# The act tiles of the experts' down pass move from SyncE's DMA queue to ScalarE's

## The chip, the cores and the metric

One Trainium2 chip, one of its cores. The metric is the device time of one execution in microseconds (us), as the median of several runs. Engines are named as in the profile: PE is TensorE (matmul), PEld its weight load, DVE VectorE, ACT ScalarE, POOL GpSimd, SP SyncE; SPq is SyncE's own row of issued transfers.

## The reference, cut to what matters

The program computes three transformer blocks one after the other on 512 tokens of width 1024. The change lies in the second block's feed-forward layer, a layer of 16384 experts of which every token picks 16 for each of 8 heads:

```python
def block(args):
    hb, ib, gb = args
    act = jax.nn.gelu(jnp.einsum('pd,phkd->phk', hb, expert_u[ib]))
    return jnp.einsum('phk,phkd->pd', gb.astype(hb.dtype) * act, expert_v[ib])
```

## The kernel before

For 384 of the 512 tokens the kernel works densely. The 16384 experts form 128 tiles of 128 experts. `experts_up` computes gelu(u h) of all experts of a tile for the 384 tokens and stores it as an act tile of 128 x 384 float32 in DRAM (`acts`), and it stores a matrix of gates (`gates`), zero where a token didn't pick an expert. `experts_down`, the stage of the change, then walks over the 128 tiles and sums V tile (128 experts x 1024) times (act tile x gates) in PSUM. For the other 128 tokens it gathers rows of V by index: GpSimd issues 128 indirect transfers, one for each of 128 picked slots, and VectorE adds each into `sums`, about one in a tile's time.

For tile n of `experts_down` the engines do the following, in this order on each.

- ScalarE waits for V tile n and for PE to be done with tile n-2, casts V into `v.hi`, waits for `product` of tile n, casts it into `w.hi`.
- VectorE waits for act tile n (and the gates of its group of 8 tiles) and multiplies them into `product` (L2426); it then waits for `v.hi` and computes the rest `v.lo` (helper line L71), then waits for `w.hi` and computes `w.lo` (L71), and then adds one gathered row (L2409).
- PE waits for `v.lo` and `w.lo` and makes 8 x 3 matmuls of 384 columns (L2385).
- SyncE waits for `v_ready` of tile n, fetches V tile n+3 into the slot that has come free, then act tile n+3; after every eighth tile it fetches the gates of a whole group of 8 tiles, two groups ahead. V tiles, act tiles and gates stand in one queue, in that order of issue.

The ring of V tiles has three slots (`picked.tables`), that of act tiles three (`act_ring`), that of gates two (`gate_ring`). A V tile is waited for on one of three semaphores (`v_landed`), an act tile on one of three (`act_landed`). The gates' transfer reads pieces of 1024 bytes, an act tile's reads pieces of 1536 bytes, a V tile's pieces of 4096 bytes. The fetches stand in these lines of the kernel before:

```python
nc.sync.dma_start(self.tables[:, (n + NKEYS) % 3, :], self.p.dram["peer_v"][n]).then_inc(self.v_landed[n % 3], 16)
nc.sync.dma_start(act_ring[:, n % RING3, :], acts[n]).then_inc(act_landed[n % RING3], 16)
```

Ahead of the loop SyncE issues act tile 0, the gates of tiles 0 and 1, act tiles 1 and 2, the gates of tiles 2 to 7 and those of the second group; V tiles 0 to 2 are fetched by the stage before.

Of the kernel before, what the change touches and what calls it, by code (L numbers as in the profile page):

```python
# [880 lines left out]
NKEYS = 128  # L881
# [220 lines left out]
def second_block(p, x, mod):  # L1102

    nc, d = p.nc, p.dram
    with ExitStack() as ctx:
# [25 lines left out]
        with ExitStack() as c:  # L1131
# [8 lines left out]
            gates = nc.dram_tensor("peer_gates", (LOTS, P, NKEYS, LOT_TOKENS), F32, kind="Internal").ap()  # L1140
            experts_up(p, h2, scores, acts, gates, picked)
        experts_down(p, acts, gates, x, gt2, picked)


# [1167 lines left out]
def experts_down(p, acts, gates, x, gate, picked):  # L2312
# [3 lines left out]
    nc, d = p.nc, p.dram  # L2316
    RING3 = 3
    with ExitStack() as ctx:
        ring, landed = picked.tables, picked.v_landed
        act_ring = p.sb(ctx, "act_ring", [P, RING3, DENSE])  # L2320
# [7 lines left out]
        act_landed = p.sems(ctx, *[f"act_landed{u}" for u in range(RING3)])  # L2328
        gate_landed = p.sems(ctx, "gate_landed0", "gate_landed1")
        v_hi_ready, v_ready, multiplied, w_hi_ready, w_ready, tile_done, added = p.sems(  # L2330
            ctx, "v_hi_ready", "v_ready", "multiplied", "w_hi_ready", "w_ready", "tile_done", "added")
# [10 lines left out]
        def slot(n):  # L2342
            return ring[:, (n + NKEYS) % RING3, :]

        def fetch_act(n):
            nc.sync.dma_start(act_ring[:, n % RING3, :], acts[n]).then_inc(act_landed[n % RING3], 16)

        def fetch_gates(m, first, last, landed_):
            nc.sync.dma_start(gate_ring[:, m % 2, :, first:last, :], gates[:, :, m * GATE_TILES + first:m * GATE_TILES + last, :]
                              .rearrange("l p a t -> p l a t")).then_inc(landed_, 16)  # L2350
# [9 lines left out]
        @block.sync  # L2360
        def _(sp):
            for n in range(NKEYS - RING3):
                sp.wait_ge(v_ready, n + 1)
                picked.fetch_v(n + RING3)
                sp.wait_ge(multiplied, n + 1)
                fetch_act(n + RING3)
                m = n // GATE_TILES
                if n % GATE_TILES == GATE_TILES - 1 and m + 2 < NKEYS // GATE_TILES:
                    fetch_gates(m + 2, 0, GATE_TILES, gate_landed[m % 2])

        @block.gpsimd
# [20 lines left out]
        @block.scalar  # L2392
        def _(act):
            nc.scalar.activation(share[:], picked.pre[:], ACT.Gelu_apprx_tanh).then_inc(gelu_ready, 1)
            for n in range(NKEYS):
                act.wait_ge(landed[n % RING3], 16 * (n // RING3 + 1))
                if n >= 2:
                    act.wait_ge(tile_done, n - 1)
                nc.scalar.activation(v.hi[:, n % 2, :], slot(n), ACT.Copy).then_inc(v_hi_ready, 1)  # L2399
                act.wait_ge(multiplied, n + 1)  # L2400
                nc.scalar.activation(w.hi[:, n % 2, :], product[:, n % 2, :], ACT.Copy).then_inc(w_hi_ready, 1)

        @block.vector
        def _(dve):
# [846 lines left out]
```

## Time and profile before

| | us |
|---|---|
| median of 3 runs | 4329.05 |
| lowest and highest | 4323.47, 4330.01 |
| profiled execution, its own time | 4340.69 |
| span of the profiled execution | 4338.9 |
| first and last matmul of the changed stage's sum, from the span's start | 2544.5, 3124.5 |
| PE busy over the span | 3790.5 (87%) |

The span runs from the first to the last instruction of the profiled execution; it lies 1.8 us under that execution's own time, and that execution was 11.6 us longer than the median of the runs. Times in rows are counted from the span's start. An idle time in square brackets stands at the instruction that ended it, with the engine or transfer that released it.

### The profile page before, as it was taken

Reading aid. Unit: us, or ns where it says so; the run is one execution under the profiler, and the core shown is the slowest. Engines: PE = TensorE matmul, PEld = TensorE weight load, DVE = VectorE, ACT = ScalarE, POOL = GpSimd, SP = SyncE. Lnnn points to the kernel's source line nnn. Section 1 sums busy time; section 2 is a strip of 40 time slices with the busy share of each in tenths; the row PEclk is TensorE's granted clock in tenths of the full one; section 3 lists DMA queues with packets and bytes.
Section 4 is the critical chain, followed back from the end, with each engine's and each line's share of the span. In section 5 each row is a group of like instructions: output and inputs, shape, how many; then the busy total and the mean of one; then the engine's idle time right before and its main releaser. Section 6 shows DMA issues by size and latency. Waiting matters only on the chain. (4 is left out here: it accounts for less than half of the span.)

```text
span 4338.9 us, 51551 instructions
## 1 busy us (share of the span) xinstructions
PE 3790.5 (87%) x19109; PEld 3261.0 (75%) x19109; DVE 2528.5 (58%) x4080; ACT 1207.0 (28%) x2101; POOL 348.2 (8%) x276
## 2 busy tenths in 40 slices
PE   7998977799986988889999979999877879779998
PEld 6876764478755787689999979999856848566876
DVE  4544778454434563369999867777643436654433
ACT  1101122121012232233578833333221122412300
POOL 0000011000000020002212212222100000000000
PEclk9999978799998989999999989999988979889999
DMA  3222710222211001238889889998612101021232
GB/s 140 97 71 82 255 60 1 95 74 96 73 64 58 29 1 40 87 119 271 293 291 330 307 302 329 324 336 314 220 58 73 51 33 67 1 78 68 87 104 71
DMA packets 198386, 590.94 MB, mean 136 GB/s; under 512 B 22448, under 2 KB 80688, under 8 KB 196016
## 3 DMA queue, kind: packets, MB, share of 16 engines
q1 hardware_dynamic: 161344, 454.38, 30.3%
q0 software_dynamic: 36864, 134.23, 8.7%
q8 instruction: 106, 1.74, 0.2%
q14 instruction: 72, 0.59, 0.0%
HBM read 536.11 MB, written 52.43 MB: 136 GB/s over the span
## 5 line engine op out<-in xcount | busy, mean ns | idle before, releaser
L350 DVE CAST w_hi<-w_ring 128x1024 fp32r<-128x1024 f32 (+1 forms) x336 | 238.5, 710 | 644.0 <-PE banks L315 495.8
L71 DVE TENSOR_TENSOR w_lo<-w_ring,w_hi 128x1024 fp32r<-128x1024 f32 (+1 forms) x336 | 424.5, 1263 | 11.5
L315 PE MATMUL banks<-x_hi,w_hi 128*128 128x512 f32 x896 | 355.8, 397 | 46.9 <-DVE x_lo L71 46.8
L2385 PE MATMUL out_ps<-w_hi,v_hi 128*128 128x384 f32 x1024 | 349.2, 341 | 45.5 <-DVE w_lo L71 45.5
L2085 PE MATMUL up_ps<-h_hi,u_hi 128*128 128x384 f32 x1024 | 351.4, 343 | 21.2 <-DVE u_lo L71 21.2
L315 PE MATMUL banks<-x_lo,w_hi 128*128 128x512 f32 x896 | 354.4, 396 | 0.0
L315 PE MATMUL banks<-x_hi,w_lo 128*128 128x512 f32 x896 | 354.2, 395 | 0.0
L2385 PE MATMUL out_ps<-w_hi,v_lo 128*128 128x384 f32 x1024 | 347.6, 339 | 0.0
L2385 PE MATMUL out_ps<-w_lo,v_hi 128*128 128x384 f32 x1024 | 347.6, 339 | 0.0
L2085 PE MATMUL up_ps<-h_lo,u_hi 128*128 128x384 f32 x1024 | 343.8, 336 | 0.0
L2085 PE MATMUL up_ps<-h_hi,u_lo 128*128 128x384 f32 x1024 | 343.6, 336 | 0.0
L315 PE MATMUL banks<-h_hi,w_hi 128*128 128x512 f32 x576 | 235.3, 408 | 48.5 <-DVE w_lo L71 24.2
L315 PE MATMUL banks<-hidden_hi,w_hi 128*128 128x512 f32 x608 | 239.9, 395 | 20.0 <-DVE w_lo L71 20.0
L315 PE MATMUL banks<-hidden_lo,w_hi 128*128 128x512 f32 x608 | 239.2, 393 | 0.0
L315 PE MATMUL banks<-hidden_hi,w_lo 128*128 128x512 f32 x608 | 238.8, 393 | 0.0
L315 PEld LDWEIGHTS banks<-x_hi,w_hi 128*128 128x128 f32 x896 | 169.6, 189 | 91.7 <-DVE w_lo L71 28.8
L2385 PEld LDWEIGHTS out_ps<-w_hi,v_hi 128*128 128x128 f32 x1024 | 196.6, 192 | 50.4 <-DVE v_lo L71 50.4
L315 PE MATMUL banks<-hn_hi,w_hi 128*128 128x264 f32 (+1 forms) x704 | 186.4, 324 | 52.6 <-DVE w_lo L71 45.2
L2399 ACT ACTIVATE v_hi<-expert_tiles 128x1024 fp32r<-128x1024 f32 x128 | 135.7, 1060 | 345.4 <-PE out_ps L2385 260.9
L315 PE MATMUL banks<-h_lo,w_hi 128*128 128x512 f32 x576 | 231.7, 402 | 0.0
L315 PE MATMUL banks<-h_hi,w_lo 128*128 128x512 f32 x576 | 231.0, 401 | 0.0
L2085 PEld LDWEIGHTS up_ps<-h_hi,u_hi 128*128 128x128 f32 x1024 | 193.7, 189 | 25.9 <-DVE u_lo L71 25.7
(532 smaller groups left out, 7812.0 us busy)
## 6 DMA issues: line engine op xcount, KB each, us to landing
expert_tiles<-peer_u SPq DMA_DIRECT2D x128, 512.0 KB
expert_tiles<-peer_v SPq DMA_DIRECT2D x128, 512.0 KB
w_ring<-w_in SPq DMA_DIRECT2D x104, 512.0 KB, 3.6
w_ring<-ffn_up SPq DMA_DIRECT2D x88, 512.0 KB, 3.5
w_ring<-w_ff SPq DMA_DIRECT2D x64, 512.0 KB, 3.8
ada_ring<-w_ada SPq DMA_DIRECT2D x48, 512.0 KB, 5.2
peer_acts<-act_ring SPq DMA_DIRECT2D x128, 192.0 KB
peer_gates<-staging SPq DMA_DIRECT2D x12, 2048.0 KB
```

Source lines behind the costliest of these rows:

```text
L71: return nc.vector.tensor_tensor(self.lo[at], value, self.hi[at].bitcast(F32), ALU.subtract)
L315: last = nc.tensor.matmul(banks[:, j, s, 0:n], a[:, u % 2, k, :], b[:, g * kg + k, x_from + c:x_from + c + n], start=(g == 0 and k == 0 an ...
L350: nc.vector.tensor_copy(w_parts.hi[:, u % 2], ring[:, u % slots]).then_inc(hi_ready, 1)
L2085: last = nc.tensor.matmul(up_ps[:, n % 3, 0:DENSE], a[:, n % 2, k, :], b[:, k, P:T], start=(k == 0 and part_ == 0), stop=(k == DB - 1 and ...
L2385: last = nc.tensor.matmul(out_ps[:, b, P:T], a[:, n % 2, b * P:b * P + P], r[:, n % 2, :], start=(n == 0 and part == 0), stop=(n == NKEYS ...
L2399: nc.scalar.activation(v.hi[:, n % 2, :], slot(n), ACT.Copy).then_inc(v_hi_ready, 1)
```

## The change

SyncE no longer fetches act tiles inside the loop. ScalarE issues the fetch of act tile n+3 right behind its cast of `product` of tile n, for which it has already waited until `product` n was computed, so that the slot is free. V tiles and gates stay on SyncE, and SyncE waits for `multiplied` only ahead of the gates. The act tiles 0 to 2 stay on SyncE. No computation is changed.

```diff
@@ -2362,10 +2362,9 @@
             for n in range(NKEYS - RING3):
                 sp.wait_ge(v_ready, n + 1)
                 picked.fetch_v(n + RING3)
-                sp.wait_ge(multiplied, n + 1)
-                fetch_act(n + RING3)
                 m = n // GATE_TILES
                 if n % GATE_TILES == GATE_TILES - 1 and m + 2 < NKEYS // GATE_TILES:
+                    sp.wait_ge(multiplied, n + 1)
                     fetch_gates(m + 2, 0, GATE_TILES, gate_landed[m % 2])
@@ -2399,6 +2398,8 @@
                 nc.scalar.activation(v.hi[:, n % 2, :], slot(n), ACT.Copy).then_inc(v_hi_ready, 1)
                 act.wait_ge(multiplied, n + 1)
                 nc.scalar.activation(w.hi[:, n % 2, :], product[:, n % 2, :], ACT.Copy).then_inc(w_hi_ready, 1)
+                if n + RING3 < NKEYS:
+                    nc.scalar.dma_start(act_ring[:, n % RING3, :], acts[n + RING3]).then_inc(act_landed[n % RING3], 16)
```

On SyncE, around one fetch of gates (`gate_ring`), the kernel before issues:

```order
L1895 DMA expert_tiles<-peer_v 128x1024
L2346 DMA act_ring<-peer_acts 128x384
L2349 DMA gate_ring<-peer_gates 128x12x256
L1895 DMA expert_tiles<-peer_v 128x1024
L2346 DMA act_ring<-peer_acts 128x384
L1895 DMA expert_tiles<-peer_v 128x1024
L2346 DMA act_ring<-peer_acts 128x384
```

At the same place the changed kernel issues on SyncE (x8 stands for eight equal rows):

```order
L1895 DMA expert_tiles<-peer_v 128x1024 x8
L2349 DMA gate_ring<-peer_gates 128x12x256
L1895 DMA expert_tiles<-peer_v 128x1024 x8
```

The act tiles have left SyncE's queue; the gates stand directly behind a V tile, and the next V tile directly behind the gates.

On ScalarE, in the middle of the stage, two tiles of the kernel before read:

```order
L2399 ACTIVATE v_hi<-expert_tiles 128x1024
L2401 ACTIVATE w_hi<-product 128x384
L2399 ACTIVATE v_hi<-expert_tiles 128x1024
L2401 ACTIVATE w_hi<-product 128x384
```

and two tiles of the changed kernel, whose lines are numbered by its own file:

```order
L2398 ACTIVATE v_hi<-expert_tiles 128x1024
L2400 ACTIVATE w_hi<-product 128x384
L2402 DMA act_ring<-peer_acts 128x384
L2398 ACTIVATE v_hi<-expert_tiles 128x1024
L2400 ACTIVATE w_hi<-product 128x384
L2402 DMA act_ring<-peer_acts 128x384
```

ScalarE has one more instruction in a tile, between its cast of `product` and its next cast of V. The order on PE, VectorE and GpSimd is the same as before.

## Rows read from the trace of the kernel before

**Rows 1.** The page's head and part 1, the whole span.

```profile
span 4338.9 us, 51551 instructions
PE 3790.5 (87%) x19109; PEld 3261.0 (75%) x19109; DVE 2528.5 (58%) x4080; ACT 1207.0 (28%) x2101; POOL 348.2 (8%) x276
```

**Rows 2.** Who waited for whom, 2530 to 3140: total us, times, longest.

```profile
ACT v_hi L2399 <- PE out_ps L2385: 260.9, 96, 5.0
ACT v_hi L2399 <- DMA expert_tiles<-peer_v: 84.3, 28, 7.3
...
DVE product L2426 <- DMA act_ring<-peer_acts: 58.0, 15, 6.7
PEld out_ps L2385 <- DVE v_lo L71: 50.4, 17, 15.2
...
DVE sums L2409 <- DMA gathered<-peer_v,expert_ids: 4.1, 1, 4.1
```

**Rows 3.** Two bursts to the next; columns: engines' busy, PEclk, DMA, GB/s.

```profile
2689.60:2727.60 38.00, 34.78 (x192) 34.49 (x192) 26.85 (x33) 12.00 (x16) 8.01 (x8) 0.96 0.92 319
2762.80:2797.70 34.90, 33.30 (x192) 33.01 (x192) 26.53 (x33) 12.00 (x16) 8.01 (x8) 1.00 0.95 328
```

**Rows 4.** SyncE's timeline around one fetch of gates: start, us taken to issue.

```profile
2762.05 0.43 SPq L2346 DMA_DIRECT2D act_ring<-peer_acts  x1
2762.82 0.39 SPq L2349 DMA_DIRECT2D gate_ring<-peer_gates  x1
2765.83 2.39 SPq L1895 DMA_DIRECT2D expert_tiles<-peer_v  x1
2768.27 0.49 SPq L2346 DMA_DIRECT2D act_ring<-peer_acts  x1
```

**Rows 5.** The same burst in stretches of 2 us; columns as in rows 3.

```profile
2764.00:2766.00 2.00, 2.00 (x14) 2.00 (x13) 1.42 (x2) 0.89 (x2) 0.59 (x1) 1.00 0.78 250
...
2776.00:2778.00 2.00, 2.00 (x13) 2.00 (x12) 0.00 (x0) 0.07 (x1) 0.94 (x1) 1.00 1.02 402
```

**Rows 6.** ScalarE's timeline, three bursts, with the idle time before each.

```profile
2706.96 1.06 ACT L2399 ACTIVATE v_hi<-expert_tiles 128x1024 fp32r<-128x1024 f32 x1 [6.97 <-DMA expert_tiles<-peer_v]
...
2742.28 1.06 ACT L2399 ACTIVATE v_hi<-expert_tiles 128x1024 fp32r<-128x1024 f32 x1 [3.98 <-DMA expert_tiles<-peer_v]
...
2764.38 0.51 ACT L2401 ACTIVATE w_hi<-product 128x384 fp32r<-128x384 f32 x1
2767.57 1.06 ACT L2399 ACTIVATE v_hi<-expert_tiles 128x1024 fp32r<-128x1024 f32 x1 [2.69 <-PE out_ps L2385]
...
2777.93 1.06 ACT L2399 ACTIVATE v_hi<-expert_tiles 128x1024 fp32r<-128x1024 f32 x1 [4.72 <-DMA expert_tiles<-peer_v]
```

**Rows 7.** VectorE's timeline at the same three bursts.

```profile
2707.49 0.56 DVE L2426 TENSOR_TENSOR product<-act_ring,gate_ring 128x384 f32<-128x384 f32 x1 [4.92 <-DMA act_ring<-peer_acts]
...
2744.11 0.56 DVE L2426 TENSOR_TENSOR product<-act_ring,gate_ring 128x384 f32<-128x384 f32 x1 [3.23 <-DMA act_ring<-peer_acts]
...
2779.25 0.56 DVE L2426 TENSOR_TENSOR product<-act_ring,gate_ring 128x384 f32<-128x384 f32 x1 [3.46 <-DMA act_ring<-peer_acts]
```

**Rows 8.** PE's weight loads that ended three pauses.

```profile
2565.27 0.29 PEld L2385 LDWEIGHTS out_ps<-w_hi,v_hi 128*128 128x128 f32 x1 [5.05 <-DVE v_lo L71]
...
2709.93 0.19 PEld L2385 LDWEIGHTS out_ps<-w_hi,v_hi 128*128 128x128 f32 x1 [3.51 <-DVE v_lo L71]
...
2781.53 0.19 PEld L2385 LDWEIGHTS out_ps<-w_hi,v_hi 128*128 128x128 f32 x1 [1.89 <-DVE v_lo L71]
```

**Rows 9.** PE and PEld at L2385 behind the last two pauses, PEclk, DMA, GB/s.

```profile
2710.00:2720.00 10.00, 10.00 (x49) 10.00 (x50) 0.83 0.84 276
2781.60:2791.60 10.00, 10.00 (x58) 10.00 (x59) 1.00 0.92 322
```

**Rows 10.** Transfers issued in the stage, with the size of each.

```profile
act_ring<-peer_acts SPq DMA_DIRECT2D x128, 192.0 KB
gate_ring<-peer_gates SPq DMA_DIRECT2D x15, 1536.0 KB
```

## The prediction

> **What bounds the kernel now.** I read the page's engine shares first: PE is busy for 87% of the span [rows 1], so only what PE waits for counts. Then the stage of the change alone, by its table of waits. PE's weight loads waited 50.4 us there, all of it for `v_lo` [rows 2]; the longest, 15.2 us, ends at the stage's first matmul, which leaves 35.2 us between tiles. That is the reachable idle time, 0.8% of the kernel. One step back the table names the cause: ScalarE waited 84.3 us for V tiles and VectorE 58.0 us for act tiles, while the gathered rows, which travel in GpSimd's own queue, were late once, by 4.1 us [rows 2]. When nothing is late, ScalarE waits for PE (260.9 us, 96 times [rows 2]), and a tile takes 4.16 us of PE (8 tiles take 33.3 us, PE's busy time in the second of [rows 3]).
>
> The timelines then show where the 35 us lie. There are 14 fetches of gates in the loop and one pause of PE behind each, plus one of 5.05 us at tile 3 [rows 8], where two sets of gates are under way at once. The 14 pauses add up to 29.4 us, 1.0 to 3.5 us each, the longest of them in [rows 8]. [Rows 4] show one: the gates (1536 KB) are issued at 2762.82, and the V tile behind them in the queue at 2765.83. That V tile starts ScalarE's cast at 2777.93 [rows 6], 12.1 us after its issue, and PE resumes at 2781.53 [rows 8]. The granted clock is the second price of a pause. Behind the pause of 1.89 us it stayed at 1.00 and 59 weight loads ran in 10 us; behind the one of 3.51 us it was 0.83 in the mean, so part of the time at the lower level, 1.2 GHz, and only 50 loads ran [rows 9]. Nine loads of 0.17 us (10 us over 59) are 1.5 us. This happened behind 5 of the 14 pauses, and 38.0 us against 34.9 us from one fetch of gates to the next is what it and the longer pause make together [rows 3].
>
> **What the change removes: the lateness of act tiles.** In the loop `product` stands ahead of `v_lo` on VectorE, so a late act tile holds `v_lo`. But `v_lo` also needs ScalarE's 1.06 us cast of V, and only what `product` ends after that cast counts (a hand-over of 0.1 us taken off). At the three bursts of [rows 6, 7]:
> - 2707.49 + 0.56 = 2708.05 against 2706.96 + 1.06 + 0.1 = 2708.12: nothing.
> - 2744.67 against 2743.44: 1.23 us.
> - 2779.81 against 2779.09: 0.72 us.
> The same subtraction at all 14 bursts gives 7.7 us, 0.55 us each, and 1.05 us at tile 3. So of the 58.0 us of waiting for act tiles only 8.7 us held PE; the rest ran beside the wait for V, which the change leaves behind the gates. This is the first point that I want seen: the V tile that is late stands in the same place of the same queue as before.
>
> **What it adds: act tiles that overtake.** During a burst the DMA engines are full: their share is 1.02, at 402 GB/s, late in the burst [rows 5]. An act tile is 192 KB [rows 10], 196,608 bytes, so 0.49 us at 400 GB/s (my estimate from these rows). Before, the late V tile n+4 had act tile n+3 ahead of it in the queue, and acts n+4, n+5 and n+6 behind it. Now ScalarE issues act n+4 behind its cast at 2764.38, act n+5 one tile later and act n+6 two tiles later, at about 2773, all before the V tile lands at 2777.9 [rows 6]. They compete with it: +0.49, +0.49, and for the last, which meets only the V tile's end, half, +0.25. Act n+3 leaves the burst, since it is issued about 1.6 us sooner (behind the cast of `product` instead of behind `v_lo`), where the engines have room (share 0.78, 250 GB/s just after the gates are issued [rows 5]): -0.49. SyncE comes to the gates one issue of 0.43 us sooner [rows 4]; I count half of it, since what goes ahead of the gates at that time is not full bandwidth: -0.2. Sum for V: +0.54 us a burst. The bounds are 0 (the acts fit into the unused share at the start of the burst) and +0.98 (all three in full, no gain from the earlier gates).
>
> **The rest of the edit** I cost at nothing. ScalarE issues 125 transfers of about the 0.43 us that SyncE takes for one [rows 4]; the 2.69 us for which ScalarE then waits for PE covers it [rows 6]. If that cover is gone, it is 0.43 us a tile, but it is gone only right behind a pause, where the next cast of V may start 0.4 us late and PE has a whole tile of 4.16 us in hand. No transfer is issued by ScalarE in this trace, so there's no row for it; the bounds are 0.1 us and SyncE's blocked issue of 2.39 us [rows 4], which 2.69 us still cover. SyncE's removed waits cost nothing: it issues and waits on, and of what it issues only V matters.
>
> **The sum.** 14 x 0.54 = +7.6 us for V, -7.7 us for acts; at tile 3, +1.5 us (three acts overtake) - 1.05 us = +0.4 us; clock unchanged. Together +0.3 us. The profiled execution would go from 4340.69 to 4341; the median of the runs is 11.6 us lower, and I put the change on it: 4329 us. What a measurement of this kernel can tell from no change is about 0.2%, 8.7 us, so 4320.4 and 4337.7 are the borders.
>
> The Trainium skill, DMA: Bandwidth & Descriptors, section "Issuing engines are not separate DMA queues", says that transfers issued by different engines share the same 16 DMA engines and interleave, and that using several only saves issue time. By that rule alone the sum is 0, 4329 us; no run here shows it yet for ScalarE's queue. It speaks against a gain from bandwidth, not against a gain from order.
>
> **The rivals.**
> - Faster: the acts hide in the unused share at the head of the burst, V lands when it did, and all of the acts' lateness is gone. For it: 0.78 of the share used for 2 us [rows 5], which at 400 GB/s leaves room for 0.3 MB, one and a half act tiles. Against: acts n+5 and n+6 come when the share is full. It gives -8.7 us and spares the slower clock behind one or two pauses (-1.5 to -3): 4329 - 11 = 4318 us. Chance 0.22. It decides where V is later by less than 0.1 us a burst.
> - Slower: the overtaking acts cost V their full price, 0.98 us a burst. For it: the gathered rows in their own queue are hardly ever late [rows 2], so a queue of its own does win over SyncE's backlog, and the loser is the V tile that all wait for. 14 x 0.98 - 7.7 + 0.4 = +6.4 us, and longer pauses bring the slower clock behind three more, +4.5 us: 4340 us. Chance 0.17. It decides from about 0.8 us a burst. The skill's page of above, section "Queues, rings and completion order", says that each DMA engine goes round its queues in turn, a packet from each; by that rule acts would pass the gates' backlog, as this rival says.
> - Slower by ScalarE: if its issue blocks behind the gates for longer than SyncE's 2.39 us, v_hi is late before the pause comes. Beyond the 2.69 us each us is paid once a burst, at most about 1 us: 4329 + 14 = 4343 us. Against: SyncE's blocked issue is of its own queue's backlog. Chance 0.05.
> - Nothing changes: acts stay behind the gates also from the other queue, both landings as before: 4329 us. Chance 0.08. My forecast, the wash, has 0.48.
>
> **How the numbers follow.** Wash and nothing make 0.56 for within 0.2%; faster 0.22; slower 0.17 + 0.05 = 0.22. The range takes in both main rivals with their bounds: 4314 to 4342 us. It leaves out somewhat under 2 in 10: a gain of more than the 8.7 us and the clock, and a blocking ScalarE.
>
> **What would show it.** In the changed trace the wait of `product` for act tiles should be near nothing, and that of `v_hi` for V tiles should grow from 84.3 us by 5 to 10 us, with as many pauses of PE as before, behind the gates, 27 to 32 us in 14. If V's wait stays or falls, the faster rival holds; if PE's pauses pass 36 us, the slower. ScalarE waiting for PE for less than 200 us would show that its issue isn't free. I am wrong most easily in V's landing: it is set by the slowest of 16 engines, and 0.3 us a burst either way is 4 us.

## The result, and the profile after

The changed kernel is slower by half a per cent: its median is 4352.61 us against 4330.81 us before, 12 runs each, ratio 1.0049 with a 95% interval of 1.0036 to 1.0062. The prediction was 4329 us in a range of 4314 to 4342.

The page of the changed kernel, its head, part 1 and the queues of part 3:

```profile
span 4352.7 us, 51551 instructions
PE 3797.2 (87%) x19109; PEld 3271.8 (75%) x19109; DVE 2529.1 (58%) x4080; ACT 1204.9 (28%) x2101; POOL 351.1 (8%) x276
...
q1 hardware_dynamic: 143344, 429.80, 29.1%
q0 software_dynamic: 36864, 134.23, 8.7%
q10 hardware_dynamic: 18000, 24.58, 1.8%
```

Against [rows 1], PE is busy for 6.7 us more and its weight loads for 10.8 us more, with as many instructions; the other engines stay within 3 us. A third queue, q10, now carries 18000 packets and 24.58 MB: the 125 act tiles that ScalarE fetches.

The table of waits of the changed kernel, 2530 to 3160 (total us, times, longest):

```profile
ACT v_hi L2398 <- PE out_ps L2384: 273.9, 96, 6.7
DVE v_lo L71 <- ACT v_hi L2398: 168.0, 106, 6.8
ACT v_hi L2398 <- DMA expert_tiles<-peer_v: 100.5, 27, 8.4
PEld out_ps L2384 <- DVE v_lo L71: 64.5, 17, 15.4
...
DVE sums L2410 <- DMA gathered<-peer_v,expert_ids: 4.1, 1, 4.1
```

Against [rows 2], the wait of `product` for act tiles is gone altogether; that of `v_hi` for V tiles has grown from 84.3 to 100.5 us (the prediction had 5 to 10 us more), and PE's wait for `v_lo` from 50.4 to 64.5 us.

The same stretch as in the second of [rows 3], and a later one, in the changed kernel (from one fetch of gates to the next; engines' busy, PEclk, DMA share, GB/s):

```profile
2768.70:2808.20 39.50, 36.26 (x194) 35.97 (x193) 26.77 (x34) 11.89 (x16) 8.11 (x8) 0.91 0.86 295
...
2843.40:2878.30 34.90, 33.48 (x194) 33.19 (x193) 26.73 (x34) 11.89 (x16) 8.10 (x8) 1.00 0.98 348
```

The first took 34.9 us before and takes 39.5 now, with 0.91 of the clock; the later one is as long as that row of before. So the change hurts some bursts much more than others.

The first of them step by step. SyncE's timeline of the changed kernel (start, us taken to issue):

```profile
2768.28 0.33 SPq L1895 DMA_DIRECT2D expert_tiles<-peer_v  x1
2768.66 0.43 SPq L2349 DMA_DIRECT2D gate_ring<-peer_gates  x1
2772.44 0.33 SPq L1895 DMA_DIRECT2D expert_tiles<-peer_v  x1
```

ScalarE's timeline, same kernel:

```profile
2770.43 0.33 ACTq L2402 DMA_DIRECT2D act_ring<-peer_acts  x1
...
2774.59 0.33 ACTq L2402 DMA_DIRECT2D act_ring<-peer_acts  x1
...
2778.34 1.06 ACT L2398 ACTIVATE v_hi<-expert_tiles 128x1024 fp32r<-128x1024 f32 x1 [2.69 <-PE out_ps L2384]
2778.75 0.33 ACTq L2402 DMA_DIRECT2D act_ring<-peer_acts  x1
2779.31 0.51 ACT L2400 ACTIVATE w_hi<-product 128x384 fp32r<-128x384 f32 x1
2786.81 1.06 ACT L2398 ACTIVATE v_hi<-expert_tiles 128x1024 fp32r<-128x1024 f32 x1 [7.00 <-DMA expert_tiles<-peer_v]
```

VectorE's:

```profile
2782.32 0.55 DVE L2427 TENSOR_TENSOR product<-act_ring,gate_ring 128x384 f32<-128x384 f32 x1
...
2787.97 1.23 DVE L71 TENSOR_TENSOR v_lo<-expert_tiles,v_hi 128x1024 fp32r<-128x1024 f32 x1 [5.10 <-ACT v_hi L2398]
```

And PE's weight loads:

```profile
2789.78 0.28 PEld L2384 LDWEIGHTS out_ps<-w_hi,v_hi 128*128 128x128 f32 x1 [3.53 <-DVE v_lo L71]
2789.95 0.33 PEld L2384 LDWEIGHTS out_ps<-w_lo,v_hi 128*128 128x128 f32 x1
```

The V tile issued at 2772.44 starts ScalarE's cast at 2786.81, 18.15 us after the gates' issue at 2768.66; at the burst of [rows 4, 6] it was 2777.93 - 2762.82 = 15.11 us. Three act tiles are issued between gates and landing, at 2770.43, 2774.59 and 2778.75. VectorE computed `product` at 2782.32 and waited for nothing; it then stood 5.10 us for `v_hi`. PE's pause is 3.53 us, where it was 1.89 [rows 8]. Behind it the loads take 0.33 us. PE and PEld at that line in the 10 us behind the pause:

```profile
2789.80:2799.80 10.00, 9.99 (x42) 10.00 (x43) 0.70 0.77 252
```

43 loads at a granted clock of 0.70, where [rows 9] had 59 at 1.00 behind the shorter pause.

Over all 14 bursts, summed up from the same timelines ("V lands" is the mean time from the gates' issue to the start of the cast of the late V tile, the one issued next behind the gates, over the 13 or 14 bursts where the profile names that tile's transfer as what the cast waited for; long loads are weight loads of the stage over 0.25 us; the stage is from its first to its last matmul):

| | V lands | pauses of PE, 14 bursts | long loads | stage |
|---|---|---|---|---|
| before | 15.62 us | 29.5 us | 92 | 580.0 us |
| after | 17.66 us | 43.1 us | 163 | 603.9 us |

The difference is made of these two columns: 13.5 us more of pauses, and 71 more long loads, which follow each other every 0.31 us in the mean instead of every 0.17 us, 71 x 0.14 = 9.9 us. Together 23.4 us, and the stage grew by 23.9 us; its pauses outside the 14 bursts grew by the other 0.5 us. (The two profiled executions differ by only 13.8 us, since that of before was about 10 us above its median and lost them outside this stage.)

### The profile page after: what moved, and what is told of

The parts are those of the page before. It is cut to its first block and busy times, and to the rows that moved or that the text cites. A ratio compares the mean times of both kernels' runs of the same rounds, so it can differ in the third digit from the quotient of the medians.

```text
span 4352.7 us, 51551 instructions
## 1 busy us (share of the span) xinstructions
PE 3797.2 (87%) x19109; PEld 3271.8 (75%) x19109; DVE 2529.1 (58%) x4080; ACT 1204.9 (28%) x2101; POOL 351.1 (8%) x276
## 3 DMA queue, kind: packets, MB, share of 16 engines
q10 hardware_dynamic: 18000, 24.58, 1.8%
## 5 line engine op out<-in xcount | busy, mean ns | idle before, releaser
L71 DVE TENSOR_TENSOR v_lo<-expert_tiles,v_hi 128x1024 fp32r<-128x1024 f32 x128 | 156.8, 1225 | 168.9 <-ACT v_hi L2398 168.0
L2384 PEld LDWEIGHTS out_ps<-w_hi,v_hi 128*128 128x128 f32 x1024 | 199.9, 195 | 64.5 <-DVE v_lo L71 64.5
L2398 ACT ACTIVATE v_hi<-expert_tiles 128x1024 fp32r<-128x1024 f32 x128 | 135.6, 1060 | 378.3 <-PE out_ps L2384 273.9
```

The source lines that it names most:

```text
L71: return nc.vector.tensor_tensor(self.lo[at], value, self.hi[at].bitcast(F32), ALU.subtract)
L2384: last = nc.tensor.matmul(out_ps[:, b, P:T], a[:, n % 2, b * P:b * P + P], r[:, n % 2, :], start=(n == 0 and part == 0), stop=(n == NKEYS ...
```

## The experiments

The table has each run's median beside that of the kernel before on the same chip; e14 and e15 were timed once, so they have no interval. V lands and pauses are as above, from each run's profile.

| | median | before | ratio, 95% | V lands | pauses | long loads |
|---|---|---|---|---|---|---|
| act ahead of V, one queue (e1) | 4313.08 | 4327.36 | 0.9969, 0.9958 to 0.9981 | 15.46 | 16.8 | 64 |
| late issue on ScalarE (e2) | 4359.31 | 4327.36 | 1.008, 1.0061 to 1.01 | 17.29 | 38.8 | 154 |
| before, no gates (e3) | 4298.36 | 4327.36 | 0.9935, 0.9916 to 0.9954 | - | 0 | 20 |
| after, no gates (e4) | 4299.82 | 4327.36 | 0.9933, 0.9916 to 0.9951 | - | 0 | 22 |
| after, acts in two halves (e5) | 4356.59 | 4327.5 | 1.0074, 1.0056 to 1.0092 | 17.75 | 44.0 | 164 |
| after, acts a tile later (e6) | 4340.89 | 4327.5 | 1.0034, 1.002 to 1.0048 | 16.91 | 32.3 | 109 |
| before, gates on ScalarE (e7) | 4298.69 | 4327.5 | 0.9944, 0.9925 to 0.9963 | - | 1.9 | 24 |
| e1, gates in six pieces (e8) | 4293.95 | 4327.5 | 0.9923, 0.9904 to 0.9942 | - | 0 | 35 |
| e1, two transfers more, SyncE (e9) | 4353.07 | 4326.78 | 1.0047, 1.0027 to 1.0066 | 17.61 | 42.2 | 180 |
| e1, two more, ScalarE (e10) | 4359.45 | 4326.78 | 1.0065, 1.0044 to 1.0086 | 17.97 | 48.1 | 206 |
| after, half of each act (e11) | 4326.57 | 4326.78 | 0.9998, 0.9983 to 1.0012 | 16.35 | 26.0 | 71 |
| e9 without gathers (e12) | 4322.94 | 4329.13 | 0.9988, 0.9973 to 1.0002 | 16.49 | 26.5 | 49 |
| e12, four instead of two (e13) | 4360.9 | 4329.13 | 1.0077, 1.0055 to 1.0098 | 18.22 | 50.3 | 193 |
| e13, later V held back (e14) | 4350.51 | 4332.56 | timed once | 17.76 | 44.4 | 152 |
| after, later V held back (e15) | 4361.18 | 4332.56 | timed once | 17.50 | 48.6 | 145 |

My theory after the result: act tiles that pass the gates in a queue of their own make the V tile behind the gates late. The rivals: ScalarE's own issue delays its casts; a third queue is a burden in itself; the sooner issue is what hurts, whatever the queue.

**e1: the sooner issue alone, in SyncE's queue.**

```diff
             for n in range(NKEYS - RING3):
-                sp.wait_ge(v_ready, n + 1)
-                picked.fetch_v(n + RING3)
                 sp.wait_ge(multiplied, n + 1)
                 fetch_act(n + RING3)
+                sp.wait_ge(v_ready, n + 1)
+                picked.fetch_v(n + RING3)
                 m = n // GATE_TILES
```

> The changed kernel was 22 us slower. Theory A (overtaking from a queue of their own): it is ScalarE's own queue that lets act tiles pass the gates' backlog, so this kernel, which issues act tile n+3 as early as ScalarE did (as soon as product n is there, ahead of V tile n+3) but on SyncE's queue, has not the loss: 4325 to 4335 us, 14 pauses of PE of about 2.1 us, V's landing behind the gates at most 0.5 us later than before. Rival B (earliness: an act tile issued ahead of its V tile displaces it, whatever the queue): 4340 to 4355 us, pauses of about 3 us. Rival C (ScalarE's issue holds up its casts): as the kernel before.

It is faster than before, by 14 us, and 12 us below the range that theory A gave. The waits of e1:

```profile
ACT v_hi L2399 <- DMA expert_tiles<-peer_v: 80.0, 25, 7.0
...
PEld out_ps L2385 <- DVE v_lo L71: 34.4, 12, 15.3
...
DVE sums L2409 <- DMA gathered<-peer_v,expert_ids: 11.2, 3, 6.1
DVE product L2426 <- DMA act_ring<-peer_acts: 6.7, 6, 2.6
```

The acts' lateness is nearly gone (6.7 us of 58.0 in [rows 2]) and V comes when it did. Act n+4 is now ahead of V n+4, but acts n+5 and n+6 can't pass. So the sooner issue is not what hurts, and the gain that the change was open to exists: it is there when nothing overtakes. The pauses fall by more than the 7.7 us of late acts (29.5 to 16.8). The traces show one more reason: the gates are issued sooner. PE runs out of work 17.6 us behind the gates' issue in most bursts of e1, where it was 16.9 us in the mean before, so a V tile that lands as long behind the gates holds PE 0.6 us less. And 4.54 us of the 16.8 are of another kind: at one burst VectorE waited 6.1 us for a gathered row (the row above), and PE stood behind it.

**e2: the late issue, on ScalarE's queue.**

```diff
+                if n + RING3 < NKEYS:
+                    act.wait_ge(v_ready, n + 1)
+                    nc.scalar.dma_start(act_ring[:, n % RING3, :], acts[n + RING3]).then_inc(act_landed[n % RING3], 16)
```

> Acts on ScalarE's queue as in the changed kernel, but issued only once v_lo n is computed, which is when SyncE issued them before. Theory A: the queue counts, so still 4343 to 4358 us, with pauses near 3 us. Rival B (earliness): back to 4326 to 4336 us. Rival C (ScalarE's issue holds up its casts): as slow as the changed kernel or slower, as ScalarE now waits too, and its casts of V start later than PE's release in tiles far from the gates.

As slow as the change or a little slower, 1 us above the range that theory A gave. Its waits:

```profile
ACT v_hi L2398 <- DMA expert_tiles<-peer_v: 98.7, 21, 8.9
...
PEld out_ps L2384 <- DVE v_lo L71: 60.6, 17, 15.3
```

e1 and e2 are the two halves of the change: the time of issue without the queue, and the queue without the time of issue. The queue is what costs.

**e3 and e4: before and after without the gates in the loop.** Both leave out the 14 fetches; in e4 the rest is the change.

```diff
-                m = n // GATE_TILES
-                if n % GATE_TILES == GATE_TILES - 1 and m + 2 < NKEYS // GATE_TILES:
-                    fetch_gates(m + 2, 0, GATE_TILES, gate_landed[m % 2])
...
-                    dve.wait_ge(gate_landed[m % 2], 16 * (m // 2 + 1))
+                    dve.wait_ge(gate_landed[m % 2], 16)
```

> The kernel before without the 14 fetches of gates in the loop (the gates of the first two groups are used again, so that part of the computation is left out). All theories: without the backlog the 14 pauses go, 29 us, and the slower clock behind five of them, 8 us: about 4290 to 4296 us.

> The changed kernel without the 14 fetches of gates in the loop (same work left out). Theories A and B: the loss is made at the fetches of gates alone, so within 4 us of e3. Rival C (ScalarE's issue costs in every tile) or a loss of DMA rate from a third queue at any time: 10 us or more above e3.

PE and PEld at the matmul's line, over the whole stage, in the kernel before:

```profile
2544.50:3124.70 580.20, 549.59 (x3072) 544.98 (x3072) 0.97 0.89 313
```

in the changed kernel:

```profile
2537.60:3141.80 604.20, 559.69 (x3072) 555.03 (x3072) 0.95 0.88 301
```

in e3:

```profile
2542.00:3080.50 538.50, 535.77 (x3072) 535.16 (x3072) 0.99 0.87 297
```

and in e4:

```profile
2540.90:3084.90 544.00, 536.45 (x3072) 535.24 (x3072) 0.99 0.86 294
```

Without bursts the two orders give 4298.36 and 4299.82 us: all of the loss lies at the bursts, and neither ScalarE's 125 issues nor a third queue costs anything outside them. ScalarE still waits for PE 273.9 us, 96 times, in the changed kernel, against 260.9 us, 96 times [rows 2].

**e5, e6 and e11: bytes, packets and how many act tiles pass.** e5 fetches each act tile as two transfers of half its columns. e6 lets ScalarE fetch act n+2 into the slot of n-1, a tile later, so that, as I meant it, two pass instead of three. e11 fetches only the first half of the columns.

```diff
+                    for c in (0, DENSE // 2):
+                        nc.scalar.dma_start(act_ring[:, n % RING3, c:c + DENSE // 2], acts[n + RING3][:, c:c + DENSE // 2]) \
+                            .then_inc(act_landed[n % RING3], 16)
```

> The changed kernel with each act tile fetched by ScalarE in two halves of its columns: the same bytes, twice as many packets of half the size. Theory A1 (the loss is the bytes that pass V: three act tiles of 0.49 us at a burst): as the changed kernel, 4345 to 4357 us. Theory A2 (each packet of a third queue costs a turn beyond its bytes, on the slowest DMA engine above all): more than the changed kernel, 4362 us or more, pauses of 4 us and over.

```diff
+                if 1 <= n and n + RING3 - 1 < NKEYS:
+                    nc.scalar.dma_start(act_ring[:, (n - 1) % RING3, :], acts[n + RING3 - 1]).then_inc(act_landed[(n - 1) % RING3], 16)
```

> The changed kernel with ScalarE fetching act tile n+2 instead of n+3 at tile n, so that one act tile fewer passes the V tile behind the gates. Theory A1 and A2: one of three is gone, so 0.5 to 0.8 us less a burst and fewer falls of the clock: 4332 to 4345 us, unless the act tile itself is now late, which the wait of product for act tiles would show. If it doesn't matter how many pass: 4350 us or more.

```diff
+                    nc.scalar.dma_start(act_ring[:, n % RING3, 0:DENSE // 2], acts[n + RING3][:, 0:DENSE // 2]).then_inc(act_landed[n % RING3], 16)
```

> The changed kernel with act tiles of the loop fetched only in their first 192 columns (the other half of product's input stays stale, so that part of the computation is left out): half the bytes, the same number of packets and of transfers. If bytes set the loss (A1, A3): pauses fall from 3.1 us to 1.4 to 2.2 us, 4315 to 4332 us. If the number of packets or transfers sets it (A2): 4340 us or more.

The waits of e6:

```profile
ACT v_hi L2398 <- DMA expert_tiles<-peer_v: 88.9, 28, 7.1
PEld out_ps L2384 <- DVE v_lo L71: 51.0, 17, 15.2
...
DVE product L2427 <- DMA act_ring<-peer_acts: 16.6, 18, 1.8
```

and of e11:

```profile
ACT v_hi L2398 <- DMA expert_tiles<-peer_v: 81.7, 22, 8.7
PEld out_ps L2384 <- DVE v_lo L71: 47.3, 16, 15.3
```

Twice the transfers with the same bytes (e5) put V at 17.75 us, as in the changed kernel (17.66); its ratio of 1.0074 and the changed kernel's 1.0049 have intervals that overlap, so I count no difference. Half the bytes in as many transfers (e11) make the whole loss vanish. So bytes count, not the number of transfers or of pieces. And the dose is graded: V lands at 15.46 us with one act tile between gates and V (e1; 15.62 in the kernel before, where the one act tile stands just ahead of the gates), at 16.35 with three half tiles (e11), at 17.66 with three whole ones (the change). From e1 to the change that is 2.2 us for two tiles, 1.1 us each; from e11 to the change 1.3 us for the bytes of one and a half, 0.87 us each.

e6 isn't a step of this dose. ScalarE still issues three act tiles between the gates and V's landing, at about 1.8, 5.9 and 11.0 us behind the gates, where the changed kernel has 1.8, 5.9 and 10.1; each is only the tile of one number lower. V lands 0.75 us sooner than in the changed kernel, and its time lay in the range that I had expected, but the intervals of the two ratios overlap and no run shows why V came sooner.

**e7 and e8: take the burst away from V.** e7 is the kernel before with the gates issued by ScalarE; e8 is e1 with the gates of a group in six transfers of 256 KB, one a tile.

```diff
+                m = n // GATE_TILES
+                if n % GATE_TILES == GATE_TILES - 1 and m + 2 < NKEYS // GATE_TILES:
+                    nc.scalar.dma_start(gate_ring[:, m % 2], gates[:, :, (m + 2) * GATE_TILES:(m + 3) * GATE_TILES, :]
+                                        .rearrange("l p a t -> p l a t")).then_inc(gate_landed[m % 2], 16)
```

> The kernel before with the 14 fetches of gates moved to ScalarE's queue (behind its cast of product), V and act tiles staying on SyncE's. Theory A (a transfer in a queue of its own passes the other's backlog): now V and acts pass the gates, which have eight tiles of time, so the pauses go: 4292 to 4305 us. If a third queue is harmful by itself, whatever is in it, the gain is smaller: 4315 us or more.

```diff
+                m, piece = (n - GATE_TILES + 1) // GATE_TILES, (n - GATE_TILES + 1) % GATE_TILES
+                if 0 <= m and m + 2 < NKEYS // GATE_TILES and piece < 6:
+                    nc.sync.dma_start(gate_ring[:, m % 2, 2 * piece:2 * piece + 2],
...
```

> E1 (acts ahead of V, all on SyncE's queue) with the gates of a group fetched in six pieces of 256 KB, one a tile, instead of one of 1536 KB. All theories: no backlog of more than 0.65 us of transfer ahead of a V tile, so no pauses: 4290 to 4302 us, like the kernel without gates but for the 5 to 8% more bytes.

The waits of e7:

```profile
ACT v_hi L2396 <- PE out_ps L2382: 302.3, 117, 3.4
...
DVE product L2427 <- DMA act_ring<-peer_acts: 21.8, 23, 4.3
ACT v_hi L2396 <- DMA expert_tiles<-peer_v: 20.5, 9, 5.6
...
PEld out_ps L2382 <- DVE v_lo L71: 20.6, 6, 15.2
```

and of e8:

```profile
ACT v_hi L2401 <- PE out_ps L2387: 330.8, 124, 4.8
...
PEld out_ps L2387 <- DVE v_lo L71: 20.0, 3, 15.3
...
ACT v_hi L2401 <- DMA expert_tiles<-peer_v: 9.8, 2, 7.3
```

e7 uses the same third queue as the change, for the transfer that nobody waits for soon; V and acts then pass the gates, and the kernel is 0.56% faster. That refutes a third queue by itself as the cause of the loss, and shows what the choice of a queue is worth: which transfer passes which. e8 has no pause at the bursts at all and is the fastest version, 4293.95 us, 0.77% under the kernel before. It is as fast as e3 (4298.36 us), which loads no gates in the loop, while e8 loads them all.

**e9 and e10: put the overtaking back by hand.** e1 with two idle transfers of an act tile's size and shape behind each fetch of gates, in SyncE's queue (e9) or in ScalarE's one tile later (e10).

```diff
+                    for k in range(2):
+                        nc.sync.dma_start(spare[:, k, :], acts[k]).then_inc(spare_landed, 16)
```

> E1 (4313 us, 1.15 us of pause a burst) with two act tiles' worth of extra bytes (2 x 192 KB into a spare buffer, their contents unused) behind each of the 14 fetches of gates on SyncE's queue, ahead of the late V tile. Theory A1 (V is later by the bytes ahead of it and no more, 0.49 us an act tile): 14 x 0.98 = +14 us and a few falls of the clock: 4326 to 4333 us, pauses of about 2.1 us. Theory A3 (in a full burst each byte ahead of V costs about double, since gathered rows and the next tiles of V get in as well): +24 us or more, 4337 us or more, pauses of 2.8 us and over.

```diff
+                if n % GATE_TILES == 0 and 0 <= m and m + 2 < NKEYS // GATE_TILES:
...
+                        nc.scalar.dma_start(spare[:, k, :], acts[k]).then_inc(spare_landed, 16)
```

> E1 with the same two extra transfers at each burst issued on ScalarE's queue instead, one tile after the gates. If the queue only decides what passes what (A1, A3): within 4 us of e9. If a third queue has a cost of its own beyond the bytes (A2): 8 us or more above e9.

The waits of e9:

```profile
ACT v_hi L2407 <- DMA expert_tiles<-peer_v: 117.7, 30, 7.4
...
PEld out_ps L2393 <- DVE v_lo L71: 61.5, 18, 15.1
DVE product L2434 <- DMA act_ring<-peer_acts: 28.7, 15, 3.5
```

Two transfers of 192 KB ahead of V cost 40 us over e1 in SyncE's queue and 46 us in ScalarE's. The 6 us between them lie between what the two theories gave (within 4 us, or 8 us and more), and the intervals of the ratios overlap: most of the cost is the bytes', and a small one of the third queue inside a burst isn't excluded. e9 has nothing on ScalarE's queue and yet the changed kernel's time, 4353 us. V lands 2.15 us later than in e1, for two tiles that are 0.98 us of full bandwidth by the prediction's figure, so theory A1 is refuted and A3's price holds.

**e12 and e13: are the gathered rows what doubles the price?** If gathers in their own queue keep their share while the burst lasts, each act tile ahead of V lets more of them in. e12 is e9 without the gathers and without VectorE's sums, with three V tiles more behind the gates in their place; e13 has four idle act tiles instead of two.

```diff
+                    for k in range(3):
+                        nc.sync.dma_start(picked.ring[:, k, :], p.dram["peer_v"][k]).then_inc(spare_landed, 16)
+                    for k in range(2):
+                        nc.sync.dma_start(spare[:, k, :], acts[k]).then_inc(spare_landed, 16)
...
-                picked.gather(d["peer_v"].rearrange("a b n -> (a b) n"), j, j % GATHERS, gathered[j % GATHERS])
```

> E9 without GpSimd's gathers and their sums in this stage (the results of 128 tokens are left out), and with three transfers of 512 KB of V behind each fetch of gates in their stead, so that a burst holds about the bytes of e9, all in one queue: gates, three V-sized tiles, two act-sized ones, then the late V tile. It is the base for e13; alone it tells only whether such a burst pauses PE as e9 does: pauses of 1 to 3.5 us.

> E12 with four act-sized transfers at each burst instead of two, so 28 more. In e9, 28 such transfers made V land 2.15 us later a burst, over twice their 0.98 us at 400 GB/s. Theory G (the rest was the gathered row of the next tile, which GpSimd issues in the meantime and which shares the engines with the late V tile): without gathers V lands 0.9 to 1.2 us later than in e12, 14 x 1 us plus the clock: 12 to 22 us above e12. Rival H (something else that grows with the bytes, such as DMA engines getting out of step): V lands 1.8 us later or more, 30 us or more above e12.

V lands at 16.49 and at 18.22 us: 1.73 us for two act tiles with no gather under way, and e13 takes 38 us more. That is near rival H (1.8 us, 30 us or more) and far from theory G (0.9 to 1.2 us, 12 to 22 us). The price stays at about 0.9 us a tile, so the gathers don't make it, and theory G falls.

**e14 and e15: does the next V tile take bandwidth from the late one?** In both, SyncE waits at one tile of each group until the late V tile has landed before it issues the next V tile; e14 is e13 with it, e15 the changed kernel.

```diff
+                if n > GATE_TILES and n % GATE_TILES == 1:
+                    sp.wait_ge(landed[(n + 2) % RING3], 16 * ((n + 2) // RING3 + 1))
```

> E13 with SyncE holding back everything behind the late V tile (the next act tile and the next V tile) until that V tile has landed. Theory H1 (the 16 DMA engines are out of step in a full burst; the fast ones already move the next tiles and take bandwidth from the slow ones that still carry the late V tile): the late V tile lands 1 us or more sooner behind the issue of the gates than in e13, where it took 18.3 us in the mean, so 17.3 us or less. Rival H2 (the transfers behind it take nothing from it): 18.0 us or more. The span itself says little, as the next V tile is now late too.

> The changed kernel with the same hold of the next V tile on SyncE (act tiles on ScalarE run on). The late V tile landed 17.7 us behind the issue of the gates in the mean. H1: 16.9 us or less. H2: 17.4 us or more.

The late V tile lands at 17.76 us against 18.22 in e14, and at 17.50 against 17.66 in e15: 0.46 and 0.16 us sooner. In e14 that lies between the two theories (17.3 or less, 18.0 or more), in e15 with H2 (17.4 or more). So the next tile's share is at most half a us and not the whole of the missing cost; with one profiled run each nothing finer can be said. But with the next tile held back, e14 shows how a burst ends. One burst in stretches, whose gates were issued at 2829.66 (columns as in [rows 5]):

```profile
2842.00:2844.00 2.00, 2.00 (x14) 2.00 (x13) 0.21 (x1) 0.00 (x0) 0.00 (x0) 1.00 1.05 387
2844.00:2846.00 2.00, 2.00 (x13) 2.00 (x12) 0.00 (x0) 0.00 (x0) 0.00 (x0) 1.00 0.50 192
2846.00:2848.00 2.00, 1.58 (x10) 1.25 (x8) 0.36 (x1) 0.00 (x0) 0.00 (x0) 1.00 0.09 36
...
2848.20:2848.40 0.20, 0.00 (x0) 0.00 (x0) 0.00 (x0) 0.00 (x0) 0.00 (x0) 1.00 0.05 20
2848.40:2848.60 0.20, 0.00 (x0) 0.00 (x0) 0.00 (x0) 0.00 (x0) 0.00 (x0) 1.00 0.00 0
```

and ScalarE's cast at its end:

```profile
2848.89 1.06 ACT L2408 ACTIVATE v_hi<-expert_tiles 128x1024 fp32r<-128x1024 f32 x1 [8.07 <-DMA expert_tiles<-peer_v]
```

The share falls from 1.05 to 0.50 and 0.09, while the V tile is still on its way. One engine of 16 busy all the time is a share of 0.06, so by 2846 most DMA engines had finished, and the 0.05 up to 2848.4 are a single one with V's last packets.

## Why the prediction was wrong, point by point

**What bounds the kernel, and where the pauses lie: right.** PE's pauses stay behind the gates; with the gates gone they are gone (e3, e4).

**The lateness of act tiles, -7.7 us: right.** No `product` waits for an act tile in the changed kernel, and none holds `v_lo`. The size is worked out from the trace of before; no run measures it alone.

**ScalarE's issue at nothing: right.** The rows show 0.33 us each, inside the 2.69 us for which it waits for PE, also during the burst. (SyncE's V issue behind the gates took 2.39 us in [rows 4], but that is not the rule: it took 0.33 us in 9 of the 14 bursts of before and in 13 of the 14 of the changed kernel.) The issue doesn't even wait for the cast of `product` that stands ahead of it in the program: the one at 2778.75 comes while V is being cast, 0.56 us ahead of the cast of `product` at 2779.31. e4 against e3 puts it at 1.5 us for 125 issues, within their intervals. The rival of a blocking ScalarE is refuted, though not by its argument that an issue waits on its own queue's backlog: in e7 the gates are in ScalarE's queue, and SyncE's issue of the act tile, 2.4 us behind theirs, took up to 1.60 us.

**"Sum for V: +0.54 us a burst": wrong, and this is the first step that failed.** PE's pauses grew by 13.5 us although 7.7 us of act lateness had left them, so V held PE later by (13.5 + 7.7) / 14 = 1.5 us a burst. That lies outside the bounds of 0 and 0.98. The mechanism was named rightly: three act tiles pass, one leaves. The price of each was wrong. I took bytes over full bandwidth, 0.49 us; the change against e1 gives 1.1 us, e9 against e1 1.08 us, the change against e11 and e13 against e12 0.87 us. Of the smaller terms: measured from the gates' issue V came 2.04 us later, which would be two tiles at 1.0 us, three that pass less the one that leaves, with the last of them counted in full and not for half. The gates' sooner issue gave more than the 0.2 us that I had counted: PE ran out of work 16.9 us behind the gates' issue before and 17.6 us after, 0.6 us more. (The sum agrees: 2.04 less 0.55 for the acts and 0.96 for the pauses, 13.5 / 14, leaves 0.5 us.) Neither term has a run of its own. At tile 3, where I had +0.4 us, the pause went from 5.05 to 5.16 us.

**"Clock unchanged": the second step that failed.** 71 more slow loads are 9.9 us, beside 13.5 us of longer pauses. I had read rightly that a pause of 3.5 us brought the lower level behind it and one of 1.9 us did not, and then held the clock fixed while adding to all pauses. 10 of the 14 pauses now have slow loads behind them, against 5 before. The length of a pause alone doesn't decide it: one of 2.37 us had them before, and one of 3.38 us in the changed kernel, which ended at 2933.81, had none. PE and PEld at the matmul's line behind that one:

```profile
2933.80:2943.80 10.00, 9.96 (x57) 9.99 (x58) 1.00 0.87 293
```

**The rivals.** The slower one, "the overtaking acts cost V their full price", was what happened, in place and sign, at 4340 us against 4352.6: its price of 0.98 us a burst was short by half a us, and its clock, 4.5 us, by 5 us. Its sign, pauses over 36 us, is there: 43.1 us. I gave it 0.17, since I weighed it by a price that was half of the true one; with 1.0 us for each act tile the point from which it decides is passed at once. The faster one needed V to come no later, which e1 reached with the act tiles in SyncE's queue and neither the change nor e2 did with them in ScalarE's.

**The rules of the Trainium skill.** By the one cited from DMA: Bandwidth & Descriptors, "Issuing engines are not separate DMA queues", the sum would have been 0. For bandwidth the runs agree nearly: the same extra bytes cost 40 us from one queue and 46 from the other (e9, e10). It says nothing on who passes whom, which here was worth +0.5% (act tiles on ScalarE) or -0.56% (gates on ScalarE). The other, from "Queues, rings and completion order", that an engine goes round its queues in turn, agrees with e2, where act tiles in their own queue made V land 17.29 us behind the gates instead of 15.62, and with e7, where V and acts passed the gates and 1.9 us of pauses were left. The same page's section "Why a DMA increments its semaphore by 16 and not by 1" says that the engines that carry one transfer finish independently and that the transfer has landed only with the last; e14's end of a burst agrees, with 0.50 and 0.09 of the DMA share while V was still out.

**What stays open: why a tile costs twice its bytes.** A part is my rate: over a whole burst the engines moved 338 and 350 GB/s, not 400. The burst of [rows 4], from the gates' issue to V's landing, in the kernel before:

```profile
2762.80:2777.90 15.10, 15.10 (x89) 15.10 (x89) 10.58 (x13) 4.42 (x6) 3.96 (x4) 1.00 0.99 338
```

and the same one in the changed kernel:

```profile
2768.70:2786.80 18.10, 17.87 (x104) 17.55 (x102) 11.77 (x15) 4.42 (x6) 4.05 (x4) 1.00 1.00 350
```

At 338 GB/s 196,608 bytes are 0.58 us. From there to about 1.0 us, the small pieces of an act tile are excluded (e5 has twice as many, of half the size, and V lands at 17.75 us against 17.66), the gathers too (e13), and the next V tile for all but at most half a us a burst (e14, e15). That the slowest of the 16 engines falls further behind with every tile that is put in would fit e14's rows, but no run here separates it.

## What to carry to other kernels

Moving a transfer to another engine's queue changes which transfers may pass a backlog; give the private queue to the bulk transfer that nobody needs soon (e7), or cut the bulk into pieces (e8), and leave what PE waits for next with nothing in front of it. Price a byte put ahead of an awaited transfer from a pair of runs or from the wait's own growth, not from full bandwidth: here it was double. And where some of PE's pauses already have slow weight loads behind them, a lateness added to each can cost much of its length again through the clock: here 9.9 us beside 13.5 us.

## What the runs showed of the hardware that I had not expected

- A transfer of 192 KB ahead of a late one delays its landing by 0.9 to 1.1 us, where its bytes are 0.49 to 0.58 us (e9, e11, e13).
- The 16 DMA engines can end a burst far apart: in the one shown most had finished by 2846, and the last packet of the awaited tile came 2.4 us later, on one engine (e14).
- Issuing a transfer behind the gates can take far longer than its plain 0.33 to 0.43 us, whichever of the two queues holds them: in the kernel before, the slower of SyncE's two issues next behind the gates took 0.96 to 3.40 us over the 14 bursts; in e7, with the gates in ScalarE's queue, SyncE's act issue took 0.47 to 1.60 us. ScalarE's 125 issues of the changed kernel all took 0.33 to 0.35 us.
- The same kernel gains or loses half a per cent by which of two streams gets the second queue: 4298.69 us with the gates on it, 4352.61 us with the act tiles.
